# Order of work at the border of two feed-forward pairs: high parts of the finished block, bank copy, weight copy, block sum and scratch store

## The reference

```python
def _conv_ffn(u, w_up, w_conv, b_conv, w_down):      # D_FF = 2048, CONV_W = 3
    s = u.shape[1]
    a, val = jnp.split(u @ w_up, 2, axis=-1)         # [1024, 1024] @ [1024, 4096]
    ap = jnp.pad(a, ((0, 0), (CONV_W - 1, 0), (0, 0)))
    conv = b_conv
    for j in range(CONV_W):
        conv = conv + w_conv[j] * ap[:, CONV_W - 1 - j:CONV_W - 1 - j + s]
    return (jax.nn.silu(conv) * val) @ w_down

def first_block(...):
    ...
    h = h + gt1[:, None, :] * _hybrid_mixer(...)     # attention, state space, gates
    u = _modulate(h, g_ffn[l], sh2, sc2)
    h = h + gt2[:, None, :] * _conv_ffn(u, w_up[l], w_conv[l], b_conv[l], w_down[l])
    return _rmsnorm(h, g_final)
```

## Time and profile before

| | value |
|---|---|
| median of 3 runs | 2054.94 us |
| profiled execution, its time | 2056.71 us |
| profiled execution, its span | 2055.0 us |
| PE busy | 2025.0 us (99%) |
| PE weight loads busy | 1683.0 us (82%) |
| POOL busy | 1297.5 us (63%) |
| DVE busy | 1077.4 us (52%) |
| ACT busy | 647.4 us (32%) |
| mean granted clock of PE | 0.996 |

### The profile page before, as it was taken

How to read it: one execution, slowest core, us unless ns; L and a number is a source line. 1 busy time by engine, 2 the same in 40 slices (tenths; PEclk the granted TensorE clock), 3 DMA queues, 4 the chain that set the end, 5 groups by cost and what they waited for, 6 DMA issues and landing times. The chain is left out here.

```text
span 2055.0 us, 25788 instructions
## 1 busy us (share of the span) xinstructions
PE 2025.0 (99%) x10047; PEld 1683.0 (82%) x10047; DVE 1077.4 (52%) x1386; ACT 647.4 (32%) x1070; POOL 1297.5 (63%) x757
## 2 busy tenths in 40 slices
PE   7999999999999999999999999999999999999998
PEld 3888988888888877788888888888787888888888
DVE  6971255555463485665632377731554555534554
ACT  3302232223331364444400035433434433311103
POOL 2537544665255539998844556876787888858750
PEclk9999999999999999999999999999999999999999
DMA  9544545444454304333475240333133322198432
GB/s 371 125 109 142 185 136 177 142 154 139 155 178 144 113 32 144 103 96 130 155 281 198 82 156 22 123 129 118 63 122 130 116 103 91 44 344 300 144 133 82
DMA packets 184904, 293.24 MB, mean 143 GB/s; under 512 B 12792, under 2 KB 136272, under 8 KB 183760
## 3 DMA queue, kind: packets, MB, share of 16 engines
q1 hardware_dynamic: 174800, 268.53, 39.2%
q10 hardware_dynamic: 9984, 23.07, 3.0%
HBM read 211.64 MB, written 79.94 MB: 142 GB/s over the span
## 5 line engine op out<-in xcount | busy, mean ns | idle before, releaser
L949 POOL TENSOR_SCALAR w_h<-raw 128x512 fp32r<-128x512 f32 (+2 forms) x110 | 240.9, 2190 | 373.6 <-issue 147.8
L1465 PE MATMUL ps<-tb,w_h 128*128 128x512 f32 x1344 | 420.6, 394 | 2.8 <-DVE quads L2702 2.4
L1029 POOL TENSOR_TENSOR w_l<-raw,w_h 128x512 fp32r<-128x512 f32 x210 | 304.3, 1457 | 108.4 <-ACT w_h L2014 108.2
L1465 PEld LDWEIGHTS ps<-tb,w_h 128*128 128x128 f32 x1344 | 251.6, 188 | 63.6 <-DVE quads L2702 4.1
L1465 PE MATMUL ps<-tb,w_l 128*128 128x512 f32 x672 | 264.6, 394 | 0.0
L2014 ACT ACTIVATE w_h<-raw 128x512 fp32r<-128x512 f32 x210 | 131.0, 628 | 255.4 <-PE ps L1465 173.9
L951 POOL TENSOR_TENSOR w_l<-raw,w_h 128x512 fp32r<-128x512 f32 (+2 forms) x110 | 205.3, 1866 | 9.2
L1465 PE MATMUL ps<-act_h,w_h 128*128 128x512 f32 x504 | 197.0, 391 | 0.3 <-ACT quads L2043 0.2
L1465 PE MATMUL ps<-act_l,w_h 128*128 128x512 f32 x504 | 196.9, 391 | 0.0
L1465 PE MATMUL ps<-act_h,w_l 128*128 128x512 f32 x504 | 196.0, 389 | 0.0
L1465 PEld LDWEIGHTS ps<-tb,w_l 128*128 128x128 f32 x672 | 126.2, 188 | 28.2
(11 more groups left out here) (414 smaller groups left out, 4553.8 us busy)
## 6 DMA issues: line engine op xcount, KB each, us to landing
raw<-in_w_in SPq DMA_DIRECT2D x45, 1024.0 KB, 5.4
raw<-in_w_up SPq DMA_DIRECT2D x16, 1024.0 KB, 5.5
f_scratch<-r SPq DMA_DIRECT2D x16, 1024.0 KB, 7.9
gates_scratch<-quads SPq DMA_DIRECT2D x24, 512.0 KB, 7.4
r<-gates_scratch SPq DMA_DIRECT2D x12, 1024.0 KB, 6.3
ada_lo<-in_w_ada SPq DMA_DIRECT2D x16, 512.0 KB, 3.8
ada_hi<-in_w_ada SPq DMA_DIRECT2D x16, 512.0 KB, 4.2
gates_scratch<-gate_st ACTq DMA_DIRECT2D x32, 256.0 KB, 2.1
```

Source lines behind the costliest of these rows:

```text
L949: nc.gpsimd.tensor_scalar(w_h[:, k, c, :], src[:, c, :], 1.0, None, ALU.mult).then_inc(s["w_high"], 1)
L1029: nc.gpsimd.tensor_tensor(w7_l[:, SLOTS[o]], x, w7_h[:, SLOTS[o]].bitcast(F32), ALU.subtract)\
L1465: last = nc.tensor.matmul(bank_of(n, bank), w[:, SLOTS[o], c, :], x(c), start=(first and c == 0 and p == 0), stop=(c == KD // 2 - 1 and p ...
```

## The change

The order of pair 1 is used for all pairs. In every `fv` unit but the last, ACT ends with `f_high(p, 0)`, `copies(n + 1, 0)`, `f_high(p, 1)` and only then high part 6 of unit n + 1; that is new for the borders ahead of units 4, 6, 8, 10 and 12. In every `fa` unit from n = 2 on, DVE does `from_first` between the two `f_low`. SP issues the stores of a pair's f ahead of the load in the same unit, from n = 2 on. Nothing is computed differently, and no instruction is added or taken away.

```diff
@@ SP, the loop over the units @@
             for n in range(NF):
+                if n and KIND[n] == "fa":
+                    f_store(UNITS[n][2] - 1)
                 if n + 4 < 2 * KD:
                     load_up(n + 4)
...
-                elif KIND[n] == "fa":
-                    f_store(UNITS[n][2] - 1)
+                elif n == 0:
+                    f_store(0)
@@ ACT, the loop over the units, n > 0 @@
                 else:
-                    if kind == "fa" and n > 2:
-                        for cg in range(2):
-                            f_high(p - 1, cg)
                     if kind == "fv":
                         for cg in (1, 0):
                             conv_first(p, cg)
-                    if n > 2:
-                        copies(n, 0)
+                        if n > 1:
+                            copies(n, 0)
                     if more:
                         weights_high(n + 1, 0)
...
                 if n == 0:
                     copies(1, 0)
-                if n == 1:
-                    f_high(1, 0)
-                    copies(2, 0)
-                    f_high(1, 1)
+                if kind == "fv" and more:
+                    f_high(p, 0)
+                    copies(n + 1, 0)
+                    f_high(p, 1)
                 if more:
                     weights_high(n + 1, 6)
@@ DVE, the loop over the units @@
-                elif n == 2:
-                    f_low(1, 0)
+                elif kind == "fa":
+                    f_low(p - 1, 0)
                     from_first(n)
-                    f_low(1, 1)
-                elif kind == "fa":
-                    for cg in range(2):
-                        f_low(p - 1, cg)
-                    from_first(n)
+                    f_low(p - 1, 1)
```

## The result

The changed kernel takes 2058.23 us (median of 13 runs, 2056.59 to 2060.73), the kernel before 2054.23 us in the same measurement (13 runs, 2052.41 to 2056.09). The ratio is 1.0019, 95% interval [1.0012, 1.0027]: 4.0 us slower, where 1.3 us faster was forecast. The profiled execution took 2057.74 us, its span is 2056.0 us. The spans of the two profiled executions differ by 1.0 us only, because the units started at 755.64 us after the change and at 757.71 before, for reasons in the first 110 us that the change doesn't touch. From the first unit to the last instruction the changed kernel takes 3.1 us more. So stages are compared by their lengths, not by their place in the span.

The account below looks back on a forecast made before the run. PE, busy 99% of the span, was taken to bound the kernel. Unit 4's -1.29 us, with all other terms at zero, took the median 2054.94 us to 2053.7; the range was 2051.4 to 2056.6 us.

Parts of the forecast that it names:

- Unit 4 gains 1.29 us: Unit 4: the block sum comes 4 us ahead of product 4, so PE's wait goes, -1.29 us.
- High part 6 at +7.2 in even units, near +4.1 in odd ones; the odd units' sum at +9.4: Times in us from unit start; odd units' sum over at +10.1, product 4 due at +11.0, 0.9 us spare, no cost.
- The two rivals built on this margin: Odd units 5 to 13 lose 0.25 us each, 2055.0 us, chance 0.20; or 1.27 us each, 2060.0 us, chance 0.05.
- the one on the copy of bank e: Unit 4 stays late as bank e's copy takes the bank copy's place; 2054.1 to 2054.9 us, chance 0.07.
- The rule on f_low beside POOL: Unit 4: POOL's low part would wait out DVE's second f_low, its sums ending 0.6 us later than forecast.
- Unit 3 keeps its loss: Unit 3 keeps its 1.27 us, as its high part waited for POOL; 0 to 0.3 could go, 0 taken.
- Transfers: SP's stores and load: load issued 1.1 us later, 6 us spare in even units; stores land sooner; 0 us taken.
- Nothing later gives it back, since what follows is paced by PE, as unit 13 already is: After the reordered units: the whole 1.29 us gain stays in the total time.
- Slower by over 0.2%: 0.05: Whole kernel: chance 0.05 of a loss above 4.1 us, from odd units losing 1.27 us each, 2060.0 us.
- the first case: Odd units 5, 7, 9, 11 and 13 lose 0.25 us each, cancelling the gain; 2055.0 us, chance 0.20.

## Why the prediction was wrong, point by point

- *Unit 4 gains 1.29 us*: right. The sum L2701 came at 841.61, 6.4 us after the unit's start, against the forecast +6.25. ACT's timeline of the changed kernel in unit 4: the copy that feeds the sum, which ends 0.13 us ahead of it, and high part 6 (L2016) behind it:

```profile
840.88 0.60 ACT L2042 ACTIVATE quads<-ps 128x512 f32<-128x512 f32 x1 [1.06 <-PE ps L1467]
...
842.32 0.63 ACT L2016 ACTIVATE w_h<-raw 128x512 fp32r<-128x512 f32 x1
```

- *High part 6 at +7.2 in even units, near +4.1 in odd ones; the odd units' sum at +9.4*: right. They stand at +7.1, at +4.0 to +4.1, and at +9.3 to +9.4 (+8.7 in unit 13); no odd unit waited for its sum. The two rivals built on this margin did not occur, and neither did the one on the copy of bank e (at +13.5, due before +16.5).
- *The rule on f_low beside POOL* (the Trainium skill, "SBUF — State Buffer", section "Who interferes with whom"): the low part L1031 of unit 4 started 0.6 us before f_low's end and took 1.74 us. Excluded for those 0.6 us it would have taken 1.9. The rule fits to 0.2 us here; it cost little, since each f_low took 1.23 us in its new place, against 3.77 for both before.
- *Unit 3 keeps its loss*: right (20.67 us, 0.15 more than before, from the stores' new place).
- *Transfers*: here it failed. The step priced the load of the even units by when it is needed, found 6 us to spare, and took no look at the odd units, and none at what stands behind a load in SP's list. High part 6 of unit 13 at +4.1 instead of +1.1 was in the forecast, and its low part ends in the event by which SP is released. Behind that load stood four transfers with 0.4 us to spare. All that was needed was in the trace: L736's issue and 12.8 us to landing.
- *"Nothing later gives it back, since what follows is paced by PE, as unit 13 already is"*: this sentence carried the error into the sum. Unit 13 was paced by PE by 0.4 us. The last of the four transfers was issued 2.2 us later in the unit (+8.3 against +6.0) and took 0.9 us longer; of these 3.1 us 0.4 were spare, which leaves 2.7, against 2.85 measured. The half clock behind the wait, 1.7 us, was in no rival.
- *Slower by over 0.2%: 0.05*: the measured ratio is at 0.19%, just inside what I called the same, and outside the range given. The range had no room for a mechanism that I hadn't listed. Its upper end was also wider than its own words: the first case with a microsecond is 2056.0 us, not 2056.6. And the high part of unit 3 stood 6.03 us ahead of product 4, not 6.05; neither slip matters.

## What to carry to other kernels

When an instruction is held, follow every semaphore that it, or the one it feeds, raises, and on the engine that waits for it read the whole list behind the wait to the end of the stage: a queue that issues transfers passes a delay on to transfers that have nothing to do with it. The last instance of a repeated pattern needs its own look, as what follows it is not the next instance. Transfers that a stage's first product needs belong ahead of loads that wait for a buffer.

## What the runs showed of the hardware

A wait of PE can cost more than its length: behind 2.69 us of idle time the clock was granted at 0.50 for a while, and the matmuls took 1.73 us more (1.70 in the kernel without SP's part, behind 2.6 us). The half clock did not come behind 3.60 us in the profile of the kernel with the late transfers, nor behind 1.73 us with the old order at the last border, and there the matmuls took 0.12 us more; so from these profiles it can't be told in advance whether it will come. With idle matmuls in the gap the clock stayed at 1.00 in the profile, and the matmuls behind them took 0.17 us more than before.

How long the last of the four transfers of 1 MB took to land went with what was issued just ahead of it, more than with when it was issued itself. It took 12.8 to 13.8 us in the seven kernels in which the load of 512 KB was issued 0.5 us ahead of the four, and 11.4 to 11.8 us in the five in which the load was issued behind them or 5 us ahead.
